# Two neighbouring rows to a partition: expert weights fetched in 4 KB pieces, token turns that read every second column

## The reference, cut to what matters

```python
def expert_block(args):
    xb, e = args
    a = jax.nn.silu(xb @ w1[e]) * (xb @ w3[e])     # w1, w3: [32, 1024, 512]
    return a @ w2[e]                               # w2: [32, 512, 1024]
...
y = zeros.at[row_tok].add(yb * row_gate[:, None])  # each token: gate-weighted sum over its two experts
```

## Time and profile before

| | us |
|---|---|
| median of 3 runs | 3557.12 |
| lowest, highest run | 3553.43, 3560.2 |
| the profiled execution's own time | 3554.69 |
| its span, first to last instruction | 3553.0 |
| TensorE busy, share of the span | 87% |
| mean granted TensorE clock, 1 being 2.4 GHz | 0.927 |
| stage of the experts, first turn to last down product | 606.9 to 1144.9 |

### The profile page before, as it was taken

One profiled execution on the slowest core, in us unless ns is written; L12 is line 12 of the kernel. 1 busy time (PEld: TensorE's weight loads), 2 busy tenths in 40 slices (PEclk: granted clock), 3 DMA queues, 4 the chain that ended last, 5 costly groups with the idle time before them and its releaser, 6 DMA issues. The chain is left out here.

```text
span 3553.0 us, 34681 instructions
## 1 busy us (share of the span) xinstructions
PE 3077.8 (87%) x13906; PEld 1838.1 (52%) x13906; DVE 1046.0 (29%) x2162; ACT 746.7 (21%) x1627; POOL 164.0 (5%) x265
## 2 busy tenths in 40 slices
PE   6999974888887688999898999899948774888998
PEld 3448633444444655675455664465523343464674
DVE  3440622000000201254210472333025674200242
ACT  2111720000000202342200581100002210212341
POOL 0000001011111000000000120011100001000000
PEclk9999995899989899999999999999969887999999
DMA  6663441999999111200012100122233323011200
GB/s 229 232 232 131 174 153 44 380 377 384 386 386 337 60 53 32 76 1 24 1 36 72 72 2 1 45 84 97 77 108 155 129 77 124 0 42 55 76 1 24
DMA packets 244208, 441.15 MB, mean 124 GB/s; under 512 B 31420, under 2 KB 111820, under 8 KB 240725
## 3 DMA queue, kind: packets, MB, share of 16 engines
q1 hardware_dynamic: 234278, 416.81, 33.2%
q0 software_dynamic: 9776, 22.18, 1.8%
HBM read 408.73 MB, written 37.81 MB: 126 GB/s over the span
## 5 line engine op out<-in xcount | busy, mean ns | idle before, releaser
L347 PE MATMUL hyena_in_main<-hT,weight_slots 128*128 128x256 f32 (+1 forms) x1024 | 330.5, 486 | 1.4 <-PEq L988 1.4
L347 PEld LDWEIGHTS hyena_in_main<-hT,weight_slots 128*128 128x128 f32 x1024 | 194.6, 190 | 137.1 <-issue 124.0
L2006 PE MATMUL moe_ph<-expert_weights,moe_x_T 128*64 128x256 f32 x2048 | 235.8, 384 | 1.4 <-ACT moe_x_T L2159 1.4
L347 PE MATMUL swa_in_main<-hT,weight_slots 128*128 128x512 f32 (+1 forms) x576 | 189.3, 489 | 6.5 <-DMA weight_slots<-b_w_in 5.2
L2006 PEld LDWEIGHTS moe_ph<-expert_weights,moe_x_T 128*64 128x64 f32 x2048 | 144.6, 138 | 91.0 <-issue 24.7
L347 PE MATMUL mla_down_main<-hT,weight_slots 128*128 128x512 f32 (+1 forms) x448 | 168.6, 539 | 19.5 <-DMA weight_slots<-a_w_in 19.5
L1407 PE MATMUL qkv_main<-hT,weight_slots 128*128 128x512 f32 (+1 forms) x384 | 167.8, 580 | 0.9 <-PEq L988 0.9
L1198 PE MATMUL post_y<-expert_weights,hT 128*128 128x512 f32 x384 | 165.1, 592 | 0.0
L2023 PE MATMUL moe_py<-expert_weights,moe_act_T 128*64 128x512 f32 x512 | 161.4, 789 | 0.5 <-ACT moe_act_T L2166 0.5
L347 PEld LDWEIGHTS swa_in_main<-hT,weight_slots 128*128 128x128 f32 x576 | 110.0, 191 | 86.3 <-issue 73.7
L1996 PE MATMUL moe_px<-const_identity,moe_x 64*128 64x64 f32 x512 | 71.1, 294 | 90.1 <-DMA moe_x<-scr_tokens,moe_index 90.1
(11 more groups left out here) (357 smaller groups left out, 4117.4 us busy)
## 6 DMA issues: line engine op xcount, KB each, us to landing
expert_weights<-w SPq DMA_DIRECT2D x96, 2048.0 KB, 15.0
first_w_out<-w_mod SPq DMA_DIRECT2D x12, 2048.0 KB
expert_weights<-w_mod SPq DMA_DIRECT2D x12, 2048.0 KB, 8.0
weight_slots<-w_in SPq DMA_DIRECT2D x16, 1024.0 KB
weight_slots<-c_w_in SPq DMA_DIRECT2D x16, 1024.0 KB
weight_slots<-a_w_in SPq DMA_DIRECT2D x14, 1024.0 KB
scr_spectra<-expert_weights SPq DMA_DIRECT2D x12, 1024.0 KB, 3.8
expert_weights<-scr_spectra SPq DMA_DIRECT2D x12, 1024.0 KB, 5.3
```

The costliest lines, as they stand in the source:

```text
L347: mm = pe.matmul(main[u][0:unit.rows, 0:unit.cols], lhsT, rhs, start=(c == 0), stop=(c == r.kc - 1))
L2006: mm = pe.matmul(bank[half * T:(half + 1) * T, 0:HF], x_T[:, c, :], w[:, c, half * HF:(half + 1) * HF], start=(c == 0), stop=(c == KD - 1))
```

## The change

The first and third matrix get another layout: row index = 256g + 2p + j, so partition p takes rows 2p and 2p+1 of each block of 256 (g from 0 to 3), which lie next to each other in memory: four pieces of 4 KB to a partition instead of eight of 2 KB. The place in SBUF is the same, step c = 2g + j of the contraction at the old place of c. To match, the turn of the token rows for step c reads columns 256(c // 2) + (c % 2) + 2p: every second column of a block of 256, instead of 128 neighbouring ones. The second matrix, the products, the waits, and the number and order of DMAs stay.

```diff
-        self.w1, self.w3, self.w2 = (a[k][0].rearrange("e (c p) n -> e p c n", p=P) for k in ("w1", "w3", "w2"))
+        self.pairs1, self.pairs3 = ([t.rearrange("p (g m) -> p g m", m=2 * FF) for t in flat[k:k + 2]] for k in (0, 2))
+        self.w1, self.w3 = (a[k][0].rearrange("e (g p j) n -> e p g (j n)", p=P, j=2) for k in ("w1", "w3"))
+        self.w2 = a["w2"][0].rearrange("e (c p) n -> e p c n", p=P)
...
-        sp.dma_start(self.W1[e % 2], self.w1[e]).then_inc(Stage.w1_in[e % 2], 16)
+        sp.dma_start(self.pairs1[e % 2], self.w1[e]).then_inc(Stage.w1_in[e % 2], 16)
...
-        sp.dma_start(self.W3[e % 2], self.w3[e]).then_inc(Stage.w3_in[e % 2], 16)
+        sp.dma_start(self.pairs3[e % 2], self.w3[e]).then_inc(Stage.w3_in[e % 2], 16)
...
     for c in range(KD):
-        mm = pe.matmul(px[:, c * T:(c + 1) * T], x[:, c * P:(c + 1) * P], consts["identity"][0:T, 0:T],
+        first = c // 2 * 2 * P + c % 2
+        mm = pe.matmul(px[:, c * T:(c + 1) * T], x[:, first:first + 2 * P - 1:2], consts["identity"][0:T, 0:T],
                        start=True, stop=True)
...
-                        for dst, src in ((W1, experts.w1), (W3, experts.w3)):
-                            sp.dma_start(dst[s], src[ds(e, 1)].rearrange("o p c n -> (o p) c n"))\
+                        for dst, src in ((experts.pairs1, experts.w1), (experts.pairs3, experts.w3)):
+                            sp.dma_start(dst[s], src[ds(e, 1)].rearrange("o p g m -> (o p) g m"))\
                                 .then_inc(s_w13[s], 16)
```

## The result

The change makes the kernel slower, by a third of what was forecast. Median 3566.05 us over 8 runs against 3555.32 for the kernel before: ratio 1.0029, 95% interval 1.0018 to 1.0040. The forecast was 3587; the range reached from 3562 to 3610.

A forecast was written before the change was run, and what follows sets the result against it. The prediction took the expert rounds to be bound by the chain through gather, turn, down product and scatter, not weights. To the profiled 3554.7 us it added 20.4 (turn) and 9.0 (gather): 3584.1, as a median 3587 us; range 3562 to 3610.

The forecast's parts named there:

- ring: Chain of each expert round: down product, copy of y, scatter, next gather, its landing, turn of token rows, down product again.
- the slack of 7.9 us: Expert stage: a load of W3 landed at 1108.9 us, 7.9 us before its first product at 1116.84.
- Faster transfers: Loads of W1 and W3: 10.08 us instead of 10.84 an expert, costed at nothing since no product waits for weights.
- The turn: TensorE's turn of gathered token rows: strided reads add 0.032 us to each of 16 loads, 0.51 us a turn, 20.4 us.
- The gather: DMA of token rows: waits longer behind 4 KB weight pieces, 0.4 us in 15 rounds, times 1.5 is 9.0 us.
- the two groups: Gathers from 655 to 870 us beside W2's 4 KB pieces, median 6.9 us; from 875 beside 2 KB pieces, 6.5.
- The price of 1.5 for a us on the ring: Expert rounds: each us added before the down product costs 1.5 us, as idling lowers TensorE's clock; from two loop stretches.
- the free stride: Rival on the turn: strided reads cost nothing, only the gather's 9 us remain, 3566 us; chance 0.10.
- It does nothing: Rival on the whole change: pieces are still split, stride and gather stay in the noise, 3557 us; chance 0.06.
- A dearer stride: Rival on the turn: the full 68 ns stand in each load, + 43 + 9 us, 3609 us; chance 0.13.
- a shorter gather: Rival on the gather: shorter weight loads save 0.26 us a round, 11 us; with free stride 3546 us; chance 0.06.
- weights as the bound: Rival on the expert stage: full DMA engines bind, 0.76 us saved in each of 28 rounds, 3536 us; chance 0.03.

## Why the prediction was right or wrong, point by point

- **What bounds the kernel**: right. No weight is waited for before or after; full DMA engines did not mean late weights. The runs with a shorter ring add what the slack of 7.9 us did not say: it tells how early a load is issued, not how much rate is to spare, and with rounds only a little shorter (16.23 us from copy to copy instead of 16.40, in the run with the earlier gather and 2 KB pieces) the weights were late.
- **Faster transfers, costed at nothing**: right. 411 GB/s, loads landing nearly 4 us sooner, no gain.
- **The turn, 0.51 us and 20.4 us in all**: this is the step that failed. It measured 0.10 us, and 3.7 us in the run of the stride alone. Its bounds reached down to zero, but the value was taken from L2967, which is nearest in read but not in form: transposes, where the turn has plain fp32 products. Part of the value was not the stride's even there: L2967 itself gives 0.020 us a load, not 0.032. The doubt stood in the text, in the sentence on the rule, and was weighed too lightly. The rule of the Trainium skill, page "SBUF — State Buffer", section "Specifications (TRN2)", that two hits in 16 bytes suffice, comes close for plain products (193 ns against 188) and misses for transposes (215 against 139).
- **The gather, 0.4 us in 15 rounds and 9.0 us in all**: right in kind, about twice too large. It is some 0.1 us in all 29. The difference between the two groups, from which the 0.4 us came, was mostly not the pieces': 0.3 us of it is still there when all pieces have 4 KB. That a delay was found after all is in part luck. The pieces alone cost 3.2 and 5.5 us. What shows that bigger pieces delay a gather is the run with 8 KB, 1.1 us.
- **The price of 1.5 for a us on the ring**: 1.7 when measured by itself, 1.4 to 2.1.
- **The sum**: with the measured terms it is 31 x 0.10 = 3.1 us of turn and 29 x 0.10 = 2.9 us of gather, 6.0 us, times 1.7 is 10 us. The two measurements say 10.7 and 11.8. The interval of the price makes that 8 to 13 us, and the 0.10 us of gather is uncertain too, so the agreement to 1 us is partly chance.
- **The rivals**: the free stride, 3566 us, hit the measured 3566.05 by luck: it charges nothing for the stride, which cost 3.7 us, and 9 us for the gather, which cost 3.2 to 5.5. "It does nothing" is excluded by both intervals, which begin at 1.0018 and 1.0021. A dearer stride, a shorter gather and weights as the bound did not occur.

## What to carry to other kernels

A faster transfer is worth nothing while another chain sets the round, and a little less than nothing if that chain has small transfers in the same engines. The same edit was worth 18 us once the gather was issued earlier: so judge a layout together with what it waits behind, and after a slowdown of a few us try it again once the ring is shorter. When a price is borrowed from another line of the trace, the form of the instruction (transpose or product) has to match, not only its shape and its read.

## What the runs showed that I had not expected

- A stride of two fp32 columns adds 76 ns to a transposing load of 64x128 (139 to 215) and 5 ns to the load of a plain product (188 to 193).
- Turning 64x1024 numbers as eight transposes takes 0.71 us; as eight plain products with the identity it takes 2.00 us.
- Pieces of 8 KB in one third of the weights delay gathers beside them by 1.1 us and move no more bytes: the kernels with W2 in 4 and 8 KB pieces ran at 399 and 397 GB/s from 640 to 1100 us.
